# The passage between two blocks: row statistics in halves on ScalarE and VectorE, one scaling on GpSimd

## What is computed

```python
h = rms_norm(x, norm_g[i, 0]) * (1.0 + sc_a) + sh_a
y = moba_attention(h, ...)        # or diff_attention, conformer_conv_module
x = x + g_a * rms_norm(y, norm_g[i, 1])
h = rms_norm(x, norm_g[i, 2]) * (1.0 + sc_f) + sh_f
x = x + g_f * rms_norm(swiglu(h, ffn_w_in[i], ffn_w_out[i]), norm_g[i, 3])
```

## Time and profile before

| what | us |
|---|---|
| median of 3 runs (1019.12 to 1021.62) | 1019.26 |
| the profiled execution | 1022.5 |
| span of the profiled execution | 1019.6 |
| TensorE busy in it | 974.2 (96%) |
| VectorE busy | 845.2 (83%) |
| ScalarE busy | 544.8 (53%) |
| GpSimd busy | 60.3 (6%) |

### The profile page before, as it was taken

The page is one execution under the profiler, slowest core; times in us unless marked ns, Lnnn a source line. Parts: engine busy times, 40 slices in busy tenths (PEclk is TensorE's granted clock), DMA queues, the critical chain, the costliest instruction groups (busy, mean ns, idle before and its releaser), DMA issues. The chain is left out here.

```text
span 1019.6 us, 19343 instructions
## 1 busy us (share of the span) xinstructions
PE 974.2 (96%) x6740; PEld 893.7 (88%) x6740; DVE 845.2 (83%) x1381; ACT 544.8 (53%) x1016; POOL 60.3 (6%) x102
## 2 busy tenths in 40 slices
PE   3899999999999999999999999999998999999997
PEld 2899988999999888997999999989995789999996
DVE  6779988898888869777898888889998779997775
ACT  2455545444444467554554444459997455555552
POOL 3100002000000012122200000010000000000000
PEclk9999998999999989998999999989998889999999
DMA  9999982999999865652599999974330448966641
GB/s 337 323 333 312 326 262 68 339 343 338 315 306 315 268 187 151 181 182 67 170 350 340 330 299 321 312 227 126 94 114 21 132 134 242 276 186 185 185 124 41
DMA packets 259086, 233.51 MB, mean 229 GB/s; under 512 B 7513, under 2 KB 208986, under 8 KB 259034
## 3 DMA queue, kind: packets, MB, share of 16 engines
q1 hardware_dynamic: 256256, 226.52, 73.1%
q0 software_dynamic: 1536, 4.81, 1.4%
q10 hardware_dynamic: 1242, 1.51, 0.4%
HBM read 231.75 MB, written 1.06 MB: 228 GB/s over the span
## 5 line engine op out<-in xcount | busy, mean ns | idle before, releaser
L491 PE MATMUL work<-h_hi,whi 128*128 128x256 f32 x1440 | 409.4, 284 | 6.0 <-DVE h_lo L1269 5.1
L1205 DVE TENSOR_TENSOR wlo<-raw,whi 128x1024 fp32r<-128x1024 f32 x286 | 347.2, 1222 | 79.8 <-ACT whi L888 79.6
L491 PE MATMUL work<-h_hi,wlo 128*128 128x256 f32 x1440 | 404.9, 281 | 0.0
L491 PE MATMUL work<-h_lo,whi 128*128 128x256 f32 x1440 | 404.9, 281 | 0.0
L888 ACT ACTIVATE whi<-raw 128x1024 fp32r<-128x1024 f32 x286 | 298.0, 1055 | 135.0 <-PE work L491 44.6
L491 PEld LDWEIGHTS work<-h_hi,whi 128*128 128x128 f32 x1440 | 273.1, 190 | 14.0 <-issue 6.9
L491 PEld LDWEIGHTS work<-h_lo,whi 128*128 128x128 f32 x1440 | 273.0, 190 | 3.1
L491 PEld LDWEIGHTS work<-h_hi,wlo 128*128 128x128 f32 x1440 | 273.9, 190 | 0.0
L1217 DVE SCALAR_TENSOR_TENSOR acc<-ada_raw,csil,acc 128x512 f32<-128x512 f32 (+1 forms) x256 | 190.8, 747 | 4.3 <-DMA ada_raw<-in_ada_w 1.4
L511 PE MATMUL Y<-whi,ab_hi 128*128 128x512 f32 x308 | 97.7, 398 | 0.0
L511 PE MATMUL Y<-whi,ab_lo 128*128 128x512 f32 x308 | 96.7, 395 | 0.0
(11 more groups left out here) (204 smaller groups left out, 1164.5 us busy)
## 6 DMA issues: line engine op xcount, KB each, us to landing
ada_raw<-in_ada_w SPq DMA_DIRECT2D x88, 512.0 KB, 6.4
raw<-in_ffn_w_in SPq DMA_DIRECT2D x88, 512.0 KB, 7.8
ada_raw<-in_mod_w SPq DMA_DIRECT2D x48, 512.0 KB, 6.4
raw<-in_ffn_w_out SPq DMA_DIRECT2D x44, 512.0 KB, 6.1
raw<-in_f_up_w SPq DMA_DIRECT2D x44, 512.0 KB, 4.5
raw<-in_moba_w_qkv SPq DMA_DIRECT2D x24, 512.0 KB, 7.7
raw<-in_diff_w_qkv SPq DMA_DIRECT2D x24, 512.0 KB, 7.4
raw<-in_a_pw_w SPq DMA_DIRECT2D x24, 512.0 KB, 5.5
```

Source lines behind the costliest of these rows:

```text
L491: mm = pe.matmul(dst, w[:, u, ws], h[:, k, :], start=(k == 0 and m == 0), stop=(k == KT - 1 and m == 2))
L1205: dve.tensor_tensor(wlo[:, u, :], raw[:, u, :], whi[:, u, :].bitcast(F32), ALU.subtract).then_inc(lo[u], 1)
```

## The change

It does four things. In `post_norm` the addition to the second tile of xt is written as two instructions of 512 columns, the first of which counts a new semaphore `x_half`. The second tile's square is split: ScalarE squares the first 512 columns after `x_half` (sum in `ssh[:, 0:1]`), VectorE the other 512 and the eps column (sum in `ssh[:, 1:2]`), and VectorE adds the two sums. The first tile of xs is computed by GpSimd in place of VectorE, between the two powers, behind a wait on its own power; the second tile of xs is computed by VectorE in two halves, each of which TensorE waits for by itself. In the last step of the feed-forwards s = 1 and 3, sums(3) stands ahead of the product. The last store is split in two as well. Stage s = 0 keeps its own way.

```diff
--- before.py
+++ after.py
@@ -159,6 +159,10 @@
                 return work[:, k // 2, (k % 2) * S:(k % 2 + 1) * S]
             return x_parts(s, k - k % 2, k - k % 2 + 2)[:, k % 2, :]
 
+        def xs_parts_before(s):
+
+            return 2 + 3 * (s - 1) if s else 0
+
         def h_parts_before(s):
 
             return 4 + 5 * (s - 1) if s else 0
@@ -166,7 +170,7 @@
         mod_bank = {s: Y[:, 3, :] if s == 0 else work[:, 3, :] for s in range(6)}
         ssx, rsx = small[:, 0:2], small[:, 4:6]
         msy, rsy = small[:, 8:10], small[:, 10:12]
-        ssy = sb("ssy", [P, 2 * TT])
+        ssy, ssh = sb("ssy", [P, 2 * TT]), sb("ssh", [P, 2])
         mhalf, eps2 = small[:, 12:13], small[:, 13:14]
         mmax, mneg = small[:, 14:18], small[:, 18:22]
         msum, mrec = small[:, 22:26], small[:, 26:30]
@@ -194,7 +198,7 @@
         par_T, cols_ready, csil_ready = sem("par_T"), sem("cols_ready"), sem("csil_ready")
         ssx_done, rsx_done = sem("ssx_done"), sem("rsx_done")
         ssy_done, msy_done, rsy_done = sem("ssy_done"), sem("msy_done"), sem("rsy_done")
-        xs_ready = sem("xs_ready")
+        xs_ready, x_half, ssh_done, ssv_done = sem("xs_ready"), sem("x_half_ready"), sem("ssh_done"), sem("ssv_done")
         hT, h32v, h32a, hhi, hlo = sem("hT"), sem("h32v"), sem("h32a"), sem("h_hi_done"), sem("h_lo_done")
         x_ready, y_done, y_tmp = sem("x_ready"), sem("y_done"), sem("y_tmp")
         mod_cols, mod_cols_used = sem("mod_cols"), sem("mod_cols_used")
@@ -390,10 +394,11 @@
                             pw2_pair(0, 2, USE[4][2])
                             pw2_pair(1, 3, USE[4][3])
                         ada_block(s // 2 + 1, NBLK - 3)
-            for t in range(TT):
-                sp.wait_ge(x_ready, 2 * LAST + t + 1)
-                sp.dma_start(out[0, t * P:(t + 1) * P, :], xt[:, t, :]).then_inc(stored, 16)
-            sp.wait_ge(stored, 16 * TT)
+            for t, a, b, done, n in ((0, 0, D, x_ready, 2 * LAST + 1), (1, 0, 512, x_half, LAST + 1),
+                                     (1, 512, D, x_ready, 2 * LAST + 2)):
+                sp.wait_ge(done, n)
+                sp.dma_start(out[0, t * P:(t + 1) * P, a:b], xt[:, t, a:b]).then_inc(stored, 16)
+            sp.wait_ge(stored, 16 * 3)
 
 
         @block.gpsimd
@@ -441,6 +446,9 @@
                 for t in range(TT):
                     pool.wait_ge(ssx_done, 2 * s + t + 1)
                     pool.tensor_tensor(rsx[:, t:t + 1], ssx[:, t:t + 1], mhalf, ALU.pow).then_inc(rsx_done, 1)
+                    if s and t == 0:
+                        pool.wait_ge(rsx_done, 2 * s + 1)
+                        pool.tensor_scalar(xs[:, 0, :], xt[:, 0, :], rsx[:, 0:1], None, ALU.mult).then_inc(xs_ready, 1)
                 if s in (2, 4):
                     pool.wait_ge(mod_gf, s // 2)
                     pool.wait_ge(hlo, h_parts_before(s + 1))
@@ -562,8 +570,10 @@
                     pe.wait_ge(mod_ga_used, s // 2 + 1)
                 need(pe, x_ready, 2 * s)
                 for t in range(TT):
-                    pe.wait_ge(xs_ready, 2 * s + t + 1)
+                    pe.wait_ge(xs_ready, xs_parts_before(s) + t + 1)
                     for k in range(KT):
+                        if s and t and k == KT // 2:
+                            pe.wait_ge(xs_ready, xs_parts_before(s) + 3)
                         if s and t == 0 and k == KT - 1:
                             pe.wait_ge(mod_cols_used, s + 1)
                         mm = pe.transpose(x_bank(s, k)[:, t * P:(t + 1) * P], xs[:, t, k * P:(k + 1) * P], ident[:])
@@ -894,8 +904,13 @@
                 for t in range(TT):
                     if s == 0:
                         act.wait_ge(x_loaded, 32)
+                    elif t:
+                        act.wait_ge(x_half, s)
+                        act.activation(xs[:, t, 0:512], xt[:, t, 0:512], ACT.Square, scale=D ** -0.5,
+                                       accum_out=ssh[:, 0:1]).then_inc(ssh_done, 1)
+                        return
                     else:
-                        act.wait_ge(x_ready, 2 * (s - 1) + t + 1)
+                        act.wait_ge(x_ready, 2 * s - 1)
                     act.activation(xs_pad[:, t, :], xt_eps[:, t, :], ACT.Square, scale=D ** -0.5,
                                    accum_out=ssx[:, t:t + 1]).then_inc(ssx_done, 1)
 
@@ -1248,12 +1263,17 @@
 
             def pre_norm(s):
                 if s:
-                    for t in range(TT):
-                        dve.wait_ge(rsx_done, 2 * s + t + 1)
-                        dve.tensor_scalar(xs[:, t, :], xt[:, t, :], rsx[:, t:t + 1], None,
-                                          ALU.mult).then_inc(xs_ready, 1)
-                        if t == 0:
-                            columns(s)
+                    half = xt_eps[:, 1, 512:D + 1]
+                    dve.wait_ge(x_ready, 2 * s)
+                    dve.scalar_tensor_tensor(xs_pad[:, 1, 512:D + 1], half, 1.0 / D, half, ALU.mult, ALU.mult,
+                                             accum_out=ssh[:, 1:2]).then_inc(ssv_done, 1)
+                    dve.wait_ge(ssh_done, s)
+                    dve.wait_ge(ssv_done, s)
+                    dve.tensor_tensor(ssx[:, 1:2], ssh[:, 0:1], ssh[:, 1:2], ALU.add).then_inc(ssx_done, 1)
+                    columns(s)
+                    dve.wait_ge(rsx_done, 2 * s + 2)
+                    for a, b in ((0, 512), (512, D)):
+                        dve.tensor_scalar(xs[:, 1, a:b], xt[:, 1, a:b], rsx[:, 1:2], None, ALU.mult).then_inc(xs_ready, 1)
                 else:
                     columns(s)
                 dve.wait_ge(mod_cols_used, s + 1)
@@ -1329,8 +1349,9 @@
                     dve.wait_ge(y_tmp, 4 * s + 2 * t + 2)
                     dve.wait_ge(rsy_done, 2 * s + t + 1)
                     yG = Y[:, 2 * t:2 * t + 2, :].rearrange("p f n -> p (f n)")
-                    dve.scalar_tensor_tensor(xt[:, t, :], yG, rsy[:, t:t + 1], xt[:, t, :], ALU.mult,
-                                             ALU.add).then_inc(x_ready, 1)
+                    for a, b, done in ((0, D, x_ready),) if t == 0 else ((0, 512, x_half), (512, D, x_ready)):
+                        dve.scalar_tensor_tensor(xt[:, t, a:b], yG[:, a:b], rsy[:, t:t + 1], xt[:, t, a:b], ALU.mult,
+                                                 ALU.add).then_inc(done, 1)
 
             def attention(s):
                 hb, rb, nb, nb3 = HEADS[s], ROWS[s], USE[s][0], USE[s][3]
@@ -1566,6 +1587,8 @@
                             prep(j, i + (nb + 1))
                         if not late_sums:
                             sums(2)
+                        if last:
+                            sums(3)
                         dve.wait_ge(used[2 + j], i + (nb + 1))
                         dve.wait_ge(gate_done, F + 1)
                         dve.tensor_tensor(act32[:, j, :], work[:, 2 * j + 1, 0:S], gate[:, j, :],
@@ -1574,7 +1597,7 @@
                             low()
                         if more:
                             prep(2 + j, i + (nb + 1))
-                        if not late_sums:
+                        if not (late_sums or last):
                             sums(3)
                     if s == 5 or not last:
                         low()
```

## The result

The changed kernel takes 1025.84 us in the median of 6 runs (1024.93 to 1029.12), the kernel before, in 6 runs, 1019.37. The ratio is 1.0059 with a 95% interval of 1.0048 to 1.0070: slower by 6 us, clear of the 0.3% that a measurement can tell. The profiled execution took 1025.44 us with a span of 1022.3.

The account below looks back on a forecast made before the run. TensorE, busy 96% of the span, bounds the kernel; only five passages leave slack. Passages -0.3, fifth +0.2, moved sum +0.2, end -0.3 sum to -0.2 us from 1019.26, forecast 1019.1 us, range 1017.1 to 1021.9.

Parts of the forecast that it names:

- rival B: Passages: GpSimd's scaling is slow, square and power of tile 1 wait for it; at 2.0 us +4.3 us, 1023.6; chance 0.15.
- the price of GpSimd's scaling: First tile of x in each passage: 1.1 us, the 0.95 us memset plus 0.18 us of a short instruction.
- upper end: GpSimd's scaling at most 2.45 us: twice the memset's 0.95 for reading and writing, plus 0.55 of a power.
- The hold of VectorE: First passage: VectorE's square waits for GpSimd's scaling to end, starting at 156.88 us where it could start at 156.67.
- my rule of 5 us for each microsecond over 1.1: Total over the passages: 5 us more for each microsecond that GpSimd's scaling takes over 1.1 us.
- buys nothing by itself: First passage: TensorE gets tile 0 at 156.88 in place of 157.17 us, but its transposes then wait for tile 1.
- passed every loss on one to one: Feed-forwards behind passages: TensorE busy 184.90 of 184.90 us, no slack, so a passage's gain or loss reaches the end.
- The moved sum: Tail of first and second feed-forward: everything slides 0.78 to 0.80 us, 0.66 saved, so +0.12 us each, +0.2 in all.
- The accumulator read and the extra sum: Split square in the passages: VectorE's accumulator read adds 0.10 us; adding the halves' sums starts at 157.76, takes 0.15 us.
- The store: Kernel's end: only 256 KB left to store saves 0.45 us, less 0.13 for the split addition, -0.3 us.
- The fifth passage: Last passage: tile 0's power comes later, so GpSimd's scaling ends later and tile 1's transposes start at 821.72, +0.2 us.
- The square's split: Passages: power of tile 1 0.20 us later than now, as accumulator read, extra sum and hold outweigh half a square.

Follow-up runs that it names:

- e8: On e1's kernel, other GpSimd instructions replaced the scaling by passage (results wrong, only times read); first product after 6.15 us with a copy, 7.33 constant, 6.42 two tensors.
- e4: Kernel before, with GpSimd scaling only 896, 768, 512, 256 and 128 columns of tile 0 in passages 1 to 5, ScalarE the rest; 1022.27 us in one execution.
- e5: Changed kernel with the square's halves swapped, VectorE squaring columns 0 to 511 and ScalarE the rest; 1025.79 us in one execution.
- e1: Kernel before plus only GpSimd's scaling of the first tile of x in the five passages; 1026.50 us against 1019.92, ratio 1.0062.
- e3: Changed kernel with ScalarE scaling the first tile in place of GpSimd, ahead of its half square; 1018.62 us against 1019.92, ratio 0.9988.

## Why the prediction was wrong

I forecast 1019.1 us and no difference; it is 1025.8 and slower, outside the range. The case that came was my rival B, GpSimd's scaling slow, at 0.15; but its size and half of its mechanism were wrong too.

**The step that failed: the price of GpSimd's scaling.** I took 1.1 us, from the memset of the earlier trace rows, and 2.45 us as the upper end. It is 2.85 us. The memset's rate holds for a copy (1.03 us, e8) and not for arithmetic: 2.5 ns a column for a tensor and a scalar (e4), and with two tensors 1.85 ns, its fixed part included (e8). The upper end was built from the memset as well, so it shared the error; the trace before held no multiplication or addition on GpSimd wider than two columns, and a bound from instructions of another kind is no bound. Nor did my range use that end: its high side stops at a scaling of 1.65 us. The Trainium skill, GPSIMD Engine Reference (4.1 Engine selection), has one-input elementwise work at roughly line rate; the copy's 1.03 us for 1024 columns agrees, the scaling's 2.85 does not.

**The hold of VectorE.** I had the square start when the scaling ends. It started at 154.65, during the scaling, and was 0.73 us long, 0.04 more than alone: it came 0.93 us after GpSimd's start, when the 0.96 us of holding were nearly over. The engines do exclude each other, in both directions (e5), but for GpSimd's scaling only in its first third. In the fifth passage the square came 0.63 us after GpSimd's start and took 1.03 us, which is the same end. The Trainium skill, SBUF — State Buffer (Who interferes with whom), has the pair held for the whole instruction by whoever issues first; it says so of VectorE's two-port modes, and of an instruction with two SBUF inputs only that it contends with a GpSimd instruction that reads SBUF. GpSimd's scaling did not hold VectorE's square for the whole instruction: 0.96 of 2.85 us. The other way round the scaling was 0.53 us longer with 0.65 us of the square still to run. That the held time is the time in which GpSimd reads its inputs is my reading; no view shows reads apart from writes.

**The path.** By my rule of 5 us for each microsecond over 1.1 the change would have cost 8.6 us. It cost 6.35, since the path is another one. The same rule at my upper end of 2.45 us gives +6.55 us, 1025.8, the measured time; that would have been luck, too low a price times too steep a rule. The square and the power of tile 1 are in time; what is late is tile 0 itself. I had written that TensorE's getting it at another time "buys nothing by itself", which was right for a scaling of 1.1 us, and I never asked from which length on tile 0 becomes the last: TensorE needs 8 transposes at 0.21 us, 1.7 us, before it comes to tile 1, so tile 0 decides once it is ready less than 1.7 us before tile 1. In e1, where square and halves are as before, the product comes after the same 7.40 us, and it moves with the length of the scaling nearly one to one in e4 and in e5's fifth passage; that shows that tile 0 decides.

**What held.** The feed-forwards passed every loss on one to one: the first two took 191.82 to 191.96 us in either kernel, from first product to the next passage, and the attention behind the second passage 118.88 and 118.89. For the convolution module behind the fourth it cannot be said, as the two traces differ by 1.5 us there. The moved sum: +0.12 us a stage forecast, +0.12 measured, and the reason stands in the timeline of VectorE: the gate's product starts 0.78 us later after the stage's first product (183.52 for 182.74), the whole chain behind it slides along, and of that the sum's old place gives back 0.66. I had called that stage one with a free DMA, and there I misread, which has a DMA share of 1.00 at 306 GB/s; no loss came of it. The accumulator read and the extra sum cost about what I gave them: the addition of the two sums starts 0.84 us after the square (0.88 forecast) and takes 0.16. The read's 0.08 us ends together with the square's 0.73 and not behind it. The store: -0.44 for -0.3, as 256 KB land in 2.0 us and not 2.15. The fifth passage was worse than the others by 0.3 us, as forecast for the same reason, GpSimd's later start.

**The square's split** was judged by the wrong company: I had it lose 0.2 us against ScalarE's whole square. Without GpSimd (e3) the power of tile 1 starts at 2.49 us in place of 2.55, a gain of 0.06 us, and with the scaling in halves the passage gains 0.33. The Vector Engine (DVE) Microarchitecture Reference of the Trainium skill (7. Points that are easy to get wrong) has such an instruction at half rate for two wide SBUF inputs; with an accumulator it ran 513 columns in 0.69 us, full rate, as I had assumed.

## What to carry to other kernels

Before work moves to GpSimd, measure that very instruction at that width: its price goes by kind (copy, two tensors, tensor and scalar stand at 1.03, 1.89 and 2.85 us for 1024 columns), and a memset in the trace says nothing of it. When a producer is swapped for a slower one, ask not only who waits for it now but how much work its consumer still has between it and the wait that ends last today; here it was 1.7 us of transposes. And look for the idle engine on the path first: ScalarE stood idle for 1 us at the right moment and did the same scaling in 1.15 us.

## What the runs showed beside that

**TensorE's clock.** In every passage of the twelve traces the granted clock falls to half (1.2 of 2.4 GHz) about the time that the statistics are computed, from 1.0 us before the addition to 3.1 us after it, while TensorE waits or multiplies by single columns. It comes back between 1.1 us before the next stage's first product and 6.4 us after it. Busy time by stretch, granted clock third from the end, from the first product on in the first passage, here of the kernel before:

```profile
161.38:163.38 2.00, 1.57 (x8) 1.24 (x9) 2.00 (x5) 1.68 (x5) 0.00 (x0) 0.91 0.00 0
163.38:165.38 2.00, 1.70 (x13) 1.30 (x12) 1.49 (x3) 1.91 (x4) 0.00 (x0) 1.00 0.00 0
```

and of e8_pool_forms:

```profile
160.01:162.01 2.00, 1.96 (x7) 1.66 (x8) 2.00 (x5) 1.69 (x5) 0.00 (x0) 0.50 0.00 0
162.01:164.01 2.00, 2.00 (x10) 2.00 (x11) 1.48 (x3) 1.91 (x4) 0.00 (x0) 0.50 0.00 0
164.01:166.01 2.00, 2.00 (x12) 2.00 (x11) 1.84 (x2) 2.00 (x3) 1.95 (x3) 0.50 0.00 0
```

Before, TensorE was back at full clock 0.4 us after the first product; there it stayed at half for over 6 us, and that feed-forward took 193.13 us in place of 191.85. The six other feed-forwards above 192 us in these traces (192.27 to 192.67) also follow a passage after which the clock stayed at half for 3.4 to 5.5 us of the stage. But two of the last feed-forwards came after 3.4 and 3.6 us of it and took their usual 191.5, and I made no run that separates the clock from other causes. It fits the scatter of 2 to 4 us between runs of one kernel, of which it may be a part. What decides how long it stays is open.

**The start.** The first passage's addition began anywhere from 152.82 to 155.89 us in the twelve traces, though what runs ahead of it is the same in all; this too is in every total.
